# Two blocks of a mixed sequence model on one core: five pairs of upward FFN tiles by seven products of quarters, convolution read from PSUM, and sums of operands at other places in the order

## The reference, cut to what matters

```python
def conv_ffn(h, w_up, conv_w, w_down):          # second block: h = rmsnorm(x, norm_ffn_gain)
    gu = causal_dwconv(h @ w_up, conv_w)        # 3 taps over time
    g, u = jnp.split(gu, 2, axis=-1)            # D_FF = 2816 columns each
    return (jax.nn.silu(g) * u) @ w_down
...
# first block, per branch a, b, c
    ua = jnp.einsum('bse,ed->bsd', ya * jax.nn.silu(ga), w_up_a[l])
    ub = jnp.einsum('bse,ed->bsd', yb * jax.nn.silu(gb), w_up_b[l])
    uc = jnp.einsum('bse,ed->bsd', yc * jax.nn.silu(gc), w_up_c[l])
    gates = jax.nn.sigmoid(gm.reshape(B, S, N_BRANCH, D))
    merged = gates[:, :, 0] * ua + gates[:, :, 1] * ub + gates[:, :, 2] * uc
```

## Time and profile before

| | us |
|---|---|
| median of 3 runs | 1230.89 |
| lowest, highest | 1230.22, 1231.79 |
| the profiled execution, its own time | 1231.38 |
| its span in the trace | 1229.3 |

### The profile page before, as it was taken

How to read it: one execution, slowest core, us unless ns; L and a number is a source line. 1 busy time by engine, 2 the same in 40 slices (tenths; PEclk the granted TensorE clock), 3 DMA queues, 4 the chain that set the end, 5 groups by cost and what they waited for, 6 DMA issues and landing times.

```text
span 1229.3 us, 18294 instructions
## 1 busy us (share of the span) xinstructions
PE 1209.8 (98%) x6667; PEld 991.1 (81%) x6667; DVE 803.1 (65%) x1283; ACT 577.4 (47%) x1132; POOL 730.4 (59%) x538
## 2 busy tenths in 40 slices
PE   9999999999998999999999999999999999999997
PEld 7987777787786899987897777878888888889886
DVE  6554427757647777646597555479999989966224
ACT  6365535676633344555644665533232323333544
POOL 8673233263358677756384557456766676886842
PEclk9999999999999999999999999999999999999999
DMA  7333221222232333364142123323333332334332
GB/s 241 104 88 84 59 69 53 61 74 74 54 86 68 86 103 96 101 185 112 53 122 61 43 71 93 103 69 103 95 86 95 102 95 82 107 88 123 107 86 69
DMA packets 62432, 112.21 MB, mean 91 GB/s; under 512 B 6857, under 2 KB 11465, under 8 KB 62345
## 3 DMA queue, kind: packets, MB, share of 16 engines
q1 hardware_dynamic: 62200, 111.06, 32.3%
q10 hardware_dynamic: 144, 0.00, 0.0%
HBM read 108.87 MB, written 2.16 MB: 90 GB/s over the span
## 4 chain that ended last, share of the span: by engine, by line
PE 76%; DVE 18%; issue 2%; ACT 2%; POOL 1%; DMA 0%; SPq 0%; DVEq 0%; POOLq 0%; ACTq 0%
PE pb L1085 17%; PE pb L1086 17%; PE pb L1088 17%; DVE cv L1955 7%; PE pb L1138 3%; PE pb L1140 3%; PE pb L1139 3%; DVE t8s L2018 2%; PE pb L1294 2%; DVE cv L1950 2%; PE pb L1270 2%; PE pb L1147 2%; DVE t7s L2018 2%; DVE zf L1943 2%; PE pb L1237 1%
## 5 line engine op out<-in xcount | busy, mean ns | idle before, releaser
L2633 POOL TENSOR_TENSOR wlo<-raw,whi 128x512 fp32r<-128x512 f32 (+2 forms) x384 | 543.1, 1432 | 329.0 <-ACT whi L1487 328.0
L1085 PE MATMUL pb<-HH,whi 128*128 128x512 f32 x856 | 345.6, 404 | 0.2 <-DVE th L1955 0.2
L1086 PE MATMUL pb<-HL,whi 128*128 128x512 f32 x856 | 338.5, 395 | 0.0
L1088 PE MATMUL pb<-HH,wlo 128*128 128x512 f32 x856 | 337.5, 394 | 0.0
L1487 ACT ACTIVATE whi<-raw 128x512 fp32r<-128x512 f32 (+2 forms) x384 | 226.0, 614 | 106.2 <-PE pb L1088 54.9
L1085 PEld LDWEIGHTS pb<-HH,whi 128*128 128x128 f32 x856 | 161.3, 188 | 42.7 <-issue 4.6
L1086 PEld LDWEIGHTS pb<-HL,whi 128*128 128x128 f32 x856 | 161.1, 188 | 38.0 <-issue 2.9
L1088 PEld LDWEIGHTS pb<-HH,wlo 128*128 128x128 f32 x856 | 160.9, 188 | 37.5
L1955 DVE SCALAR_TENSOR_TENSOR cv<-zf,vecs,cv 128x512 f32<-128x512 f32 x88 | 123.8, 1406 | 3.1
L1596 ACT ACTIVATE P<-P,stat 128x256 f32<-128x256 f32 (+3 forms) x96 | 50.6, 527 | 78.6 <-DVE stat L2196 56.2
L2633 POOL TENSOR_TENSOR fl<-cv,fh 128x512 fp32r<-128x512 f32 x22 | 32.6, 1482 | 64.3 <-ACT fh L1864 64.3
(11 more groups left out here) (460 smaller groups left out, 2560.8 us busy)
## 6 DMA issues: line engine op xcount, KB each, us to landing
raw<-in_wall SPq DMA_DIRECT2D x368, 256.0 KB, 2.7
raw<-in_wall SPq DMA_DIRECT2D x8, 260.0 KB, 3.1
X<-in_xT SPq DMA_DIRECT2D x8, 256.0 KB, 5.2
X<-in_xT SPq DMA_DIRECT2D x2, 1024.0 KB, 7.1
outT<-PP SPq DMA_DIRECT2D x8, 256.0 KB, 2.4
raw<-in_wall SPq DMA_DIRECT2D x10, 192.0 KB, 2.4
raw<-in_wall SPq DMA_DIRECT2D x9, 128.0 KB, 2.2
cst<-in_cst SPq DMA_DIRECT2D x1, 832.0 KB, 7.2
```

Of the source, the lines that this page charges most:

```text
L1085: pe.do.matmul(b, hi, xh[k], start=start, stop=False, skip_group_check=tile[0] == "down")
L1086: pe.do.matmul(b, hi, xl[k], start=False, stop=False, skip_group_check=tile[0] == "down")
L1088: m = pe.do.matmul(b, lo, xh[k], start=False, stop=stop, skip_group_check=tile[0] == "down")
L2633: g.do.tensor_tensor(lo, x, hi.bitcast(F32), ALU.subtract).then_inc(*up(name, point))
```

## The change

1. **Sums spread.** In the gate stage `t_sums` 0, 1, 2 now stand after gateA 1, gateA 3 and gateB 1, `t_parts` 0, 1, 2 after gateA 2, gateB 0 and after gateB 3 (ahead of the first `up`).
2. **Convolution from PSUM.** `conv` becomes `scaled` and `taps`. DVE multiplies the bank by `rff` in place; ACT takes the last tap out of the bank into `cv`; DVE adds the other two taps, reading the bank and `cv`. The `zf` buffers are gone. The taps of half 1, DVE's part of swish and the product of pair j now stand after `scaled` of half 0 of pair j+1.
3. **Five pairs by quarters.** The pairs j = 4, 7, 10, 13, 15 (`UPS`) are computed by seven products, in three banks: "ab" (the bank of half 0), "cd" (a third one) and "e" (half 1). Here ACT's copy to `U7` stands at S2, and PE's A12 waits for DVE's sum after it (`u2`), since A12 writes to the bank that both read. Each pair adds four weight sums, one low part and six additions of 256 columns on DVE. The finishing work of pair j-1 (`taps` 1, `product`) stands inside the pair, after A22 and ahead of S2. A fourth pair-like set of input sums is made at the start of the stage: ACT scales x into SBUF and PSUM, DVE makes four sums of 256 columns for each of four k, ACT and POOL split them. They lie in buffers in which `fh` and `fl` of j = 16 to 21 are written later.

```diff
+UPS = (4, 7, 10, 13, 15)
+NUP = NGATE + len(UPS)
...
+    elif p < NUP:
+        mat, one, two = "ffn_up", P * UPS[p - NGATE], 2816 + P * UPS[p - NGATE]
...
+        if j in UPS:
+            fm4(NGATE + UPS.index(j))
+        else:
+            fm("ffn_up", P * j)
+            fm("ffn_up", 2816 + P * j)
...
+            if x == "A22" and NGATE <= p < NUP:
+                self.add("taps", 1, UPS[p - NGATE] - 1)
+                self.add("product", UPS[p - NGATE] - 1)
...
+            if t in (1, 3):
+                add("t_sums", 0, t // 2)
+            if t == 2:
+                add("t_parts", 0, 0)
         for t in range(4):
             gate("gateB", "yB", t)
-            if t < 3:
-                add("t_parts", 0, t)
             if t < 2:
-                add("t_sums", 0, 1 + t)
+                add(("t_parts", "t_sums")[t], 0, 1 + t)
         while self.background:
             self.step()
+        add("t_parts", 0, 2)
         for i, (d, n) in enumerate(TURN):
             if i == 9:
                 gm(d, BRANCH[n])
...
+                self.pair(NGATE + UPS.index(j))
             for half in range(2):
-                take(("ffn", half, j))
-                self.proj(("ffn", half, j), "ffn_up", 2816 * half + P * j)
+                if j not in UPS:
+                    take(("ffn", half, j))
+                    self.proj(("ffn", half, j), "ffn_up", 2816 * half + P * j)
                 if j == 0 and half == 0:
                     take(("norm3",))
                     add("norm3")
-                add("conv", half, j)
-                add("swish" if half == 0 else "product", j)
+                add("scaled", half, j)
+                if half:
+                    add("taps", 0, j)
+                    add("swish", j)
+                elif j and j not in UPS:
+                    add("taps", 1, j - 1)
+                    add("product", j - 1)
+                if (j, half) in sums_of:
+                    for i in range(2):
+                        take(("ts", sums_of[j, half], i))
+                    add("t_sums", 3, sums_of[j, half])
+                if (j, half - 1) in sums_of or (j - 1, half + 1) in sums_of:
+                    add("t_parts", 3, 2 * j + half - 2)
+        add("taps", 1, NPAIR - 1)
+        add("product", NPAIR - 1)
         for kp in range(4):
             add("t_sums", 1, kp)
...
+                if kind(p) == "up":
+                    g, (xhs, xls), (ths, tls), j = 3, (hh, hl), (THU, TLU), UPS[p - NGATE]
+                    tile, half = {"A11": (("ffn", 0, j), 0), "S2": (("ffn", 0, j), 1), "S1": (("cd", j), 0), "S3": (("cd", j), 1),
+                                  "A12": (("ffn", 0, j), 0), "S4": (("ffn", 0, j), 1), "A22": (("ffn", 1, j), 0)}[x]
+                    b, starts = ps(*tile)[:, H * half:H * half + H], x in ("A11", "S1", "A22", "S4")
+                    if x == "A12":
+                        pe.wait_ge(*at("u2", p))
+                    elif x in ("A11", "S1", "A22"):
+                        free(tile)
...
+            def t_sums(g, kp):
+                if g == 3:
+                    gain = vecs("ffn_norm", kp)
...
+                    a.wait_ge(*at("full", ("wout", 7)))
+                    a.wait_ge(*at("x_ffn", 7))
+                    a.wait_ge(*at("mix_lo", 7))
+                    a.do.activation(TSU[kp][:, 0:T], xk[kp], ACT.Copy, scale=gain).then_inc(*up("a_t7"))
+                    a.do.activation(ps("ts", kp, 0)[:, H:T], xk[kp][:, H:T], ACT.Copy, scale=gain).then_inc(*up("a_t7"))
+                    a.do.activation(ps("ts", kp, 1), xk[kp + 4], ACT.Copy, scale=vecs("ffn_norm", kp + 4)).then_inc(
+                        *up("a_t7", ("t_scaled", kp)))
+
...
+                if kind(p) == "up" and x == "S2":
+                    a.wait_ge(*at("product7", p, x))
+                    a.wait_ge(*at("u3", p - 1))
+                    a.do.activation(U7, ps("ffn", 0, UPS[p - NGATE])[:, 0:H], ACT.Copy).then_inc(*up("a_c7", ("v0", p)))
...
+            def scaled(half, j):
+                o, w = cv[(3 * j + 2 * half) % 6], VEC["ffn_cw"][0] + 3 * (NPAIR * half + j) + 2
+                a.wait_ge(*at("scaled", half, j))
+                if j >= 2:
+                    a.wait_ge(*at("f_lo" if half else "product", j - 2))
+                a.do.activation(o, ps("ffn", half, j), ACT.Copy, scale=VECS[:, w:w + 1]).then_inc(
+                    *up("a_tap", ("tap", half, j)))
+
...
                     v.do.tensor_tensor(dst, one, two, op).then_inc(*up("v_t7", *points))
 
+                if g == 3:
+                    left, right = slice(0, H), slice(H, T)
+                    one, two = (ps("ts", kp, i) for i in range(2))
+                    v.wait_ge(*at("t_scaled", kp))
+                    step(x11, one[:, right], x11, ALU.subtract, ("empty", ("ts", kp, 0)))
+                    step(x12, two[:, right], x12, ALU.subtract)
+                    v.wait_ge(*last("v_t7"))
+                    step(x22, two[:, right], x11, ALU.subtract)
+                    v.wait_ge(*last("v_t7"))
+                    step(x21, two[:, left], x22, ALU.subtract, ("t_raw", g, kp), ("empty", ("ts", kp, 1)))
...
+            def product_up(p, x):
+                j, left, right = UPS[p - NGATE], slice(0, H), slice(H, T)
+                ab, cd, e = ps("ffn", 0, j), ps("cd", j), ps("ffn", 1, j)
+
+                def plus(dst, one, two, *points):
+                    v.do.tensor_tensor(dst, one, two, ALU.add).then_inc(*up("v_c7", *points))
+
+                if x == "S2":
+                    v.wait_ge(*at("v0", p))
+                    v.wait_ge(*at("product7", p, "S2"))
+                    plus(U7, ab[:, right], U7, ("u2", p))
+                elif x == "S3":
+                    v.wait_ge(*at("product7", p, "S3"))
+                    v.wait_ge(*last("v_c7"))
+                    plus(W8, cd[:, left], U7)
+                    plus(ZU, cd[:, right], U7, ("u3", p))
+                    v.wait_ge(*last("v_c7"))
+                    plus(e[:, right], cd[:, right], W8, ("empty", ("cd", j)))
+                    plus(e[:, left], e[:, left], ZU)
+                elif x == "S4":
+                    v.wait_ge(*at("product7", p, "S4"))
+                    plus(ab[:, right], ab[:, right], W8)
+
...
-            def ffn_conv(half, j):
-                n = 2 * j + half
-                z, o = zf[n % 4], cv[(3 * j + 2 * half) % 6]
-                v.wait_ge(*at("full", ("ffn", half, j)))
...
+            def scaled(half, j):
+                b = ps("ffn", half, j)
+                if j in UPS:
+                    v.wait_ge(*last("v_c7"))
+                else:
+                    v.wait_ge(*at("full", ("ffn", half, j)))
...
-                mul(z[:, 16:16 + T], ps("ffn", half, j), rff, ("empty", ("ffn", half, j)), name="v_conv")
-                v.wait_ge(*last("v_conv"))
-                if half and j >= 2:
-                    v.wait_ge(*at("f_hi", j - 2))
-                    v.wait_ge(*at("f_lo", j - 2))
-                conv(z, o, VEC["ffn_cw"][0] + 3 * (NPAIR * half + j), 3, ("conv", half, j))
+                mul(b, b, rff, ("scaled", half, j), name="v_conv")
+
+            def taps(half, j):
+                b, o, w = ps("ffn", half, j), cv[(3 * j + 2 * half) % 6], VEC["ffn_cw"][0] + 3 * (NPAIR * half + j)
+                v.wait_ge(*at("tap", half, j))
+                for i in (1, 0):
+                    d = 2 - i
+                    fused(o[:, d:T], b[:, 0:T - d], VECS[:, w + i:w + i + 1], o[:, d:T], ALU.mult, ALU.add,
+                          *[("conv", half, j), ("empty", ("ffn", half, j))] * (i == 0), name="v_conv")
+                    v.wait_ge(*last("v_conv"))
...
             def product(j):
                 o = cv[(3 * j + 2) % 6]
+                swish(j)
```

72 lines of the change are left out of this document (44 added, 28 removed).

## The result

The changed kernel takes 1244.77 us (median of 4, 1241.65 to 1247.13) against 1231.16: ratio 1.011, interval 1.0097 to 1.0123. It is 13.6 us slower where 3.5 us faster was forecast, and outside the range of 1220 to 1235. The profiled execution took 1243.45 (span 1241.6), 12.1 more than the profiled one of before. Of the six executions of experiment 1 one, a slow one, took 4770.95 us and is not in its ratio; the median there is 1227.91 with it and 1227.77 without.

The account below looks back on a forecast made before the run. PE was taken as the bound. Against the profiled 1231.38, -7.8 - 6.3 + 5 x 1.8 + 2.6 - 0.7 and 0.3 gave -3.5; from the median 1230.89 that made 1227.4 us, range 1220 to 1235.

Parts of the forecast that it names:

- the gain in the gate stage: Spreading the sums removes PE's 5.40 us wait on `yBlo` and the half clock after it: 7.8 us (bounds 4 and 8.2).
- a small wait there: Small PE wait on the earlier gate tile, put into the sum at 0.3 us.
- the first pair's extra: First upward quarter pair: input sums delay `wlo` and A12, waits 4.4 us in place of 1.8, 2.6 extra (bounds 0 and 6).
- the stall of each pair: PE waits at A12 for DVE's `u2`, ready at F + 8.8 (F: start of A11): 1.8 us taken, bounds 1.3 and 5.8.
- the half clock after new waits: PE's clock after the new stalls in the upward pairs: no cost in the sum, since 0.81 us of standing brought none.
- Views and bound: PE bounds the whole kernel, busy 1209.8 of 1229.3 us; only fewer columns or less standing of PE shorten it.
- the placing of `t_sums` 2: Gate stage: DVE makes these sums from about 374.3 to 381.3, so `yBlo` 3 comes with 1.4 us to spare.
- Rival C: Gate stage: POOL holds DVE's sums longer, `yBlo` 3 is late again; 3 to 8 us more, about 1232; chance 0.08.
- Five pairs save 6.3: Upward FFN: a pair by quarters takes PE 9.90 us instead of 11.16, 1.26 each, 6.3 for five.
- Rival D: Upward pairs: half clock follows each new stall, 2.2 us five times, 1238; chance 0.05.
- Convolution from PSUM at nothing: Upward FFN: DVE loses two operations to ACT per pair of tiles, all off PE's path, so no gain by itself.
- the tail's 0.7: First downward pair: DVE finishes the last upward product sooner, so about 0.7 us of PE's 0.97 goes (0 to 1).

Follow-up runs that it names:

- experiment 1: Changed kernel without its five quarter pairs and their input sums; spread sums and convolution from PSUM stay: 1227.91 us, ratio 0.9970 against the kernel before.
- experiments 1 and 2: The second: changed kernel without the five pairs and with gate-stage quarter sums in their old places, leaving only convolution from PSUM: 1231.06 us, ratio 0.9995.
- experiment 3: Changed kernel with swish and product of the last pair of tiles put behind product S2 instead of behind A22: 1227.49 us, ratio 0.9968.
- the repair of the gate stage: Changed kernel with `t_sums` 2 put behind gateB 3 instead of gateB 1, its parts behind the second up tile: 1243.13 us.

## Why the prediction was wrong

It forecast a gain of 3.5 us, and the profiled executions differ by a loss of 12.1. Four terms of its sum failed: the gain in the gate stage (7.8 and 0.3 for a small wait there, measured 2.5), the first pair's extra (2.6, measured 7.3), the stall of each pair (1.8, measured 2.4), and the half clock after new waits (nothing, measured 1.7).

- **Views and bound: right.** PE was the bound, and the time went where the sum had its terms: gate stage, A12 of each pair, first pair.
- **"Gain 7.8" in the gate stage: the step that failed is the placing of `t_sums` 2** "from about 374.3". It was placed by PE's tiles, each step free as soon as PE was; but gateB 1 was itself late behind the moved set 1. Measured: 2.5 up to the upward FFN (4.2 in the trace of experiment 1, where no half clock follows the wait), 3 in the runs (experiments 1 and 2). The stated bound of 4 was not reached. Rival C (0.08) came true in part: its wait was there, 2.5 us, with half clock behind it. The 0.3 for a small wait on the earlier tile went the other way: 0.2 became 1.0. A set of sums that is moved does to its new neighbour what it did to the old.
- **Five pairs save 6.3: right**, if a little low: 1.37 each where nothing waits (experiment 3), 6.9. In the changed kernel the last four take 9.9 to 10.0 beside their gap at A12 and half clock, so the sum below keeps 6.3.
- **"A stall of 1.7 to 1.8": the mechanism right, the size off**, 2.4 with the restart. A12 starts at F + 9.45 instead of 8.8: 0.2 from the pitches up to swish, 0.6 from swish held by POOL (0.9 where 0.3 was put), and the steps behind the product are some 0.2 shorter. Over four pairs that is 2.6 us. The rule of the Trainium skill ("SBUF — State Buffer", Who interferes with whom) that a DVE instruction with two SBUF inputs and a GpSimd one that reads SBUF exclude each other agrees: by it swish would end at 924.26 + 0.69 = 924.95, and it ended at 924.80. By the rule a stall was put at 2.8, and it came out at 2.4. The 0.3 was the longest such operation of before (1.02 against a median of 0.69). In that trace it is not a price but a remainder: the 28 that began with POOL idle took 0.69 to 0.70, the other 16 began with 0.45 to 0.47 left of an operation of POOL and took 1.00 to 1.02. Here 1.07 was left.
- **"2.6 extra" for the first pair: mis-sized** by 4.7: 9.7 over pace instead of 4.4 in all. The ends of the third and fourth sets were placed 3.0 and 3.7 us too early, by durations without contention in a stretch where POOL runs almost without a break; 1.85 of this is the one swish and product above. The bound (6 extra) was passed: 7.3 over another pair.
- **Half clock after the waits: missed.** Rival D had 0.05. "0.81 brought none and 5.40 did; nothing in between is shown" was true, and put all five new stalls at no cost. It is 1.7 us in the profiled execution, and the two slower ones, at a mean clock of 0.991, take 2.6 and 3.7 more.
- **Convolution from PSUM at nothing, and the tail's 0.7: right.** Ratio 0.9995; the gap at the first downward pair went from 1.08 to 0.41 us. The scaling in place in PSUM took 0.70, not 1.4.

With the measured terms the prediction's sum is: -2.5 (gate) - 6.3 + 9.7 (first pair's waits) + 9.75 (the others) + 1.7 (clock) - 0.7 = +11.7, where the profiled executions differ by 12.1. Four terms were off in the same direction, three of them for one reason: a chain over three engines was laid out at undisturbed durations or from the wrong start.

What stays open: how much of each longer time is half clock, since only one execution of each kernel has a trace. And whether the repair of the gate stage by itself is a gain: its time cannot be told from the changed kernel's.
